# Norm statistics on 32 partitions per block of 128 tokens, with an early table load and one rounding moved

## What is computed

```python
def layer_norm(x, g, b):
    mu = jnp.mean(xf, axis=-1, keepdims=True)
    var = jnp.mean(jnp.square(xf - mu), axis=-1, keepdims=True)
    return (xf - mu) * lax.rsqrt(var + LN_EPS) * g + b

def rms_norm_2(x, g):
    return xf * lax.rsqrt(jnp.mean(xf * xf, axis=-1, keepdims=True) + RMS_EPS) * g

# first stack, for each of 2 layers
x = layer_norm(ALPHA * x + token_mixing(x), ln1_g[l], ln1_b[l])
x = layer_norm(ALPHA * x + conv_ffn(x), ln2_g[l], ln2_b[l])

# second stack, for each of 2 layers
x = x + rms_norm_2(mixer(rms_norm_2(x, g[0])), g[1])
x = x + rms_norm_2(mem_cross_attention(rms_norm_2(x, g[2]), mem_n), g[3])
x = x + rms_norm_2(sqrelu_mlp(rms_norm_2(x, g[4])), g[5])
```

## Time and profile before

| what | us |
|---|---|
| median of 3 runs (3763.27 to 3771.85) | 3764.62 |
| profiled execution, its own time | 3758.41 |
| span of the profiled execution | 3756.6 |
| busy: PE / DVE / ACT / POOL in that span | 3638.1 / 1692.9 / 1495.7 / 1276.3 |

### The profile page before, as it was taken

One profiled execution on the slowest core, in us unless ns is written; L12 is line 12 of the kernel. 1 busy time (PEld: TensorE's weight loads), 2 busy tenths in 40 slices (PEclk: granted clock), 3 DMA queues, 4 the chain that ended last, 5 costly groups with the idle time before them and its releaser, 6 DMA issues.

```text
span 3756.6 us, 47739 instructions
## 1 busy us (share of the span) xinstructions
PE 3638.1 (97%) x17594; PEld 2844.2 (76%) x17594; DVE 1692.9 (45%) x2392; ACT 1495.7 (40%) x2452; POOL 1276.3 (34%) x583
## 2 busy tenths in 40 slices
PE   8999999999999999999999999999999999999997
PEld 7877787888788777778877676888744587777886
DVE  2633457443344443754325643503247564436042
ACT  3256633332323664243325544423225144344232
POOL 4422233444343222444443142444200012433442
PEclk9999999999999999999999999999999999999999
DMA  3421122223233111222222221222322200212222
GB/s 139 124 68 51 46 76 77 99 96 101 91 104 113 48 49 51 96 81 98 99 99 94 101 96 62 93 98 95 102 90 72 75 2 30 95 68 84 100 96 78
DMA packets 100867, 313.06 MB, mean 83 GB/s; under 512 B 26208, under 2 KB 26336, under 8 KB 99808
## 3 DMA queue, kind: packets, MB, share of 16 engines
q1 hardware_dynamic: 81792, 298.90, 23.6%
q10 hardware_dynamic: 18912, 11.88, 1.3%
HBM read 302.35 MB, written 5.24 MB: 82 GB/s over the span
## 4 chain that ended last, share of the span: by engine, by line
issue 45%; PE 35%; POOL 16%; DVE 2%; DMA 1%; ACT 1%; DVEq 0%; POOLq 0%; SPq 0%; ACTq 0%
POOL ring_r L2748 16%; PE ps L456 9%; PE ps L458 9%; PE ps L457 9%; PE ps L978 2%; PE ps L1078 1%; PE ps L812 1%; PE ps L997 1%; DMA ring<-in_weights 1%; PE ps L1114 0%; PE ps L1217 0%; PE ps L1166 0%; PE ps L1216 0%; DVE rounded L2646 0%; DVE Z L2646 0%
## 5 line engine op out<-in xcount | busy, mean ns | idle before, releaser
L2748 POOL TENSOR_TENSOR ring_r<-ring,rounded_r 128x1024 fp32r<-128x1024 f32 x504 | 1238.1, 2459 | 2026.1 <-ACT rounded_r L1268 2025.9
L456 PE MATMUL ps<-source_hi,rounded_r 128*128 128x512 f32 x2560 | 1015.7, 397 | 45.8 <-DVE N_lo L2326 11.1
L1268 ACT ACTIVATE rounded_r<-ring 128x1024 fp32r<-128x1024 f32 x504 | 533.5, 1059 | 1309.7 <-PE ps L458 1177.3
L457 PE MATMUL ps<-source_hi,ring_r 128*128 128x512 f32 x2560 | 1001.2, 391 | 0.0
L456 PEld LDWEIGHTS ps<-source_hi,rounded_r 128*128 128x128 f32 x2560 | 483.4, 189 | 170.0 <-DVE N_lo L2326 19.3
L458 PE MATMUL ps<-X_lo,rounded_r 128*128 128x512 f32 x1536 | 600.3, 391 | 0.0
L457 PEld LDWEIGHTS ps<-source_hi,ring_r 128*128 128x128 f32 x2560 | 483.9, 189 | 100.2 <-issue 2.4
L458 PEld LDWEIGHTS ps<-X_lo,rounded_r 128*128 128x128 f32 x1536 | 289.5, 188 | 61.0
L458 PE MATMUL ps<-N_lo,rounded_r 128*128 128x512 f32 x768 | 300.8, 392 | 0.0
L2291 DVE SCALAR_TENSOR_TENSOR T<-ps,PAR,T 128x511 f32<-128x511 f32 (+1 forms) x176 | 131.5, 749 | 227.5 <-ACT T L1483 212.6
L456 PE MATMUL ps<-H_hi,rounded_r 128*128 128x512 f32 x512 | 199.2, 389 | 0.0
(11 more groups left out here) (506 smaller groups left out, 5540.2 us busy)
## 6 DMA issues: line engine op xcount, KB each, us to landing
ring<-in_weights SPq DMA_DIRECT2D x560, 512.0 KB, 3.3
X<-in_x SPq DMA_DIRECT2D x2, 1024.0 KB, 7.0
PAIR<-Z ACTq DMA_DIRECT2D x32, 64.0 KB
out_x<-X SPq DMA_DIRECT2D x4, 512.0 KB, 2.6
SWAP<-Z ACTq DMA_DIRECT2D x4, 256.0 KB, 6.1
MEM<-in_mem ACTq DMA_DIRECT2D x1, 1024.0 KB, 4.7
mem_keys<-Z ACTq DMA_DIRECT2D x1, 1024.0 KB, 3.9
diag_in<-Y ACTq DMA_DIRECT2D x8, 128.0 KB, 2.6
```

The source lines that it names most:

```text
L456: mm(o, lh, rh, start=start, stop=False)
L457: mm(o, ll, rh, start=False, stop=False)
L1268: av(RH[:, j, :], ring[:, j, :], ACT.Copy).then_inc(w_hi, 1)
L2748: nc.gpsimd.tensor_tensor(RL[:, j, :], ring[:, j, :], RH[:, j, :].bitcast(F32), ALU.subtract).then_inc(w_lo, 1)
```

## The change

A new helper `by_block` takes the place of one matmul with 512 columns by four with 128 columns: block b of 128 tokens goes through a 128x32 part of the matrix of means to output partitions 32b to 32b+31, columns 0 to 127. The statistics then lie as 128x128 from the start. `from_block` is the loop that `spread` had, with a bank as argument.

- Layer norm: the mean is summed twice, whole in bank 4 (for `less`) and by blocks in bank 7; the mean of squares is summed by blocks in bank 5. ScalarE squares 128x128, VectorE subtracts in one instruction. `warm(7, 3)` becomes `warm(6, 2)`. One `less` moves ahead of the reciprocal.
- Output norm: sums by blocks, root and reciprocal on 128x128, and a new step `rms_spread` on TensorE whose 128x512 result stays in PSUM (bank 5 or 0), where `residual` reads it instead of `RS` in SBUF. It stands behind `values(0)` for 2 and 8, behind one `warm` for 4 and 10 (four matmuls of `warm` instead of six), behind the first chunk of keys for 6, and at the end for 12.
- Layer norm on ScalarE: the root of one element that brings the table comes ahead of square 5 instead of square 7, and the rounding of the chunk for slot 2 comes behind the square of the mean instead of ahead of it.

```diff
+            def by_block(bank, src, start, stop):
+                for b in range(ST):
+                    ins = mm(ps[b * 32:b * 32 + 32, bank, 0:P], cst("mean")[:, 0:32], src[:, b * P:b * P + P], start=start, stop=stop)
+                return ins
+            def from_block(bank):
+                for b in range(ST):
+                    row = cst("ident")[:, b * 32:b * 32 + 1].to_broadcast([P, P])
+                    ins = mm(ps[:, bank, b * P:b * P + P], row, RS[:, 0:P], start=True, stop=True)
+                return ins
             def sums(l, i):
                 mm(ps[:, 4, :], cst("mean"), RS[:], start=True, stop=False)
+                by_block(7, RS[:], True, False)
...
-                mm(ps[:, 5, :], cst("mean"), QSUM, start=True, stop=False)
+                by_block(5, QSUM, True, False)
             def sums_of(l, i, n):
-                ins = mm(ps[:, 4, :], cst("mean"), X[:, n, :], start=False, stop=last)
+                ins = by_block(7, X[:, n, :], False, last)
                 if last:
                     ins.then_inc(ln["sums"], 1)
+                mm(ps[:, 4, :], cst("mean"), X[:, n, :], start=False, stop=last)
...
-                ins = mm(ps[:, 5, :], cst("mean"), SQ[n % 2], start=False, stop=last)
+                ins = by_block(5, SQ[n % 2], False, last)
...
             def rms_out(i):
-                mm(ps[:, 5, :], cst("mean"), QS, start=True, stop=False)
+                by_block(5, QS, True, False)
                 pe.wait_ge(rms_sq, i * KT + KT)
-                mm(ps[:, 5, :], cst("mean"), SQ2[(KT - 1) % 2], start=False, stop=True).then_inc(rms_var, 1)
+                by_block(5, SQ2[(KT - 1) % 2], False, True).then_inc(rms_var, 1)
+            def rms_spread(i):
+                pe.wait_ge(rms_inv, OUT_AT[i] + 1)
+                from_block(OUT_BANK[i]).then_inc(rms_fac, 1)
...
             def squared(l, i, n):
-                if n == KT - 1:
+                if n == KT - 3:
                     av(JUNK[:], cst("eps"), ACT.Sqrt)
...
             def layer_norm(l, i, bias, following):
-                av(SQ[KT % 2], ps[:, 4, :], ACT.Square).then_inc(s["act"], 1)
+                av(SQ[KT % 2][:, 0:P], ps[:, 7, 0:P], ACT.Square).then_inc(s["act"], 1)
+                ahead(slot // RING, slot % RING)
...
-                for b in range(ST):
-                    rows, t = slice(b * 32, b * 32 + 32), slice(b * P, b * P + P)
-                    ins = tt(QSUM[rows, 0:P], ps[rows, 5, t], SQ[KT % 2][rows, t], ALU.subtract)
-                ins.then_inc(s["dve"], 1)
+                tt(QSUM[:, 0:P], ps[:, 5, 0:P], SQ[KT % 2][:, 0:P], ALU.subtract).then_inc(s["dve"], 1)
+                less(0)
                 dve.wait_ge(s["act"], at * LN_ACT + LN_STD)
                 v.reciprocal(RS[:, 0:P], RS[:, 0:P]).then_inc(s["dve"], 1)
-                less(0, 1)
+                less(1)
...
             def residual(i, lo=None):
-                inverse_root(i)
+                dve.wait_ge(rms_std, i + 1)
+                v.reciprocal(RS[:, 0:P], RS[:, 0:P]).then_inc(rms_inv, 1)
+                dve.wait_ge(rms_fac, OUT_AT[i] + 1)
...
-                        tt(N[:, t, :], N[:, t, :], RS[:], ALU.mult)
+                        tt(N[:, t, :], N[:, t, :], ps[:, OUT_BANK[i], :], ALU.mult)
```

More of the change, by code:

```diff
@@ L552, in spread @@
                 pe.wait_ge(ln["dve"], (l * 2 + i) * LN_DVE + LN_ROOT)
-                for b in range(ST):
-                    row = cst("ident")[:, b * 32:b * 32 + 1].to_broadcast([P, P])
-                    ins = mm(ps[:, 6, b * P:b * P + P], row, RS[:, 0:P], start=True, stop=True)
-                ins.then_inc(ln["sums"], 1)
+                from_block(6).then_inc(ln["sums"], 1)
             def scores(l, u):
@@ L861, in values @@
                     ins.then_inc(used, 1)
-                for c in range(RING):
+                values(0)
+                rms_spread(2 + 6 * l)
+                for c in range(1, RING):
                     values(c)
@@ L1494, in _ @@
                         squared(l, 1, c // 3)
-                    ahead(Q + (B_DOWN + c) // RING, c % RING)
+                    if c < C_DOWN - 1:
+                        ahead(Q + (B_DOWN + c) // RING, c % RING)
                     if c == 3 * RING - 1:
@@ L1628, in tail @@
                 out_tiles(B + B_MO, 4 + 6 * l, gain(l, 3), 4)
-                root(4 + 6 * l)
+                root(4 + 6 * l, 5, P)
                 split_in(2 + 3 * l, gain(l, 4))
@@ L1669, in tail @@
                                 av(N[:, n, :], N[:, n, :], ACT.Copy, scale=gain(l, 5)[:, n:n + 1])
-                root(6 + 6 * l)
+                root(6 + 6 * l, 5, P)
             act.dma_start(MN, a["mem"]).then_inc(mem_in, 16)
@@ L1745, in _ @@
             out_tiles(B_LRU_OUT, 2, gain(0, 1), bias="b_out")
-            root(2)
+            root(2, 5, P)
             tail(0)
@@ L1965, in _ @@
             out_tiles(B_RWO, 8, gain(1, 1))
-            root(8)
+            root(8, 5, P)
             tail(1)
```

19 lines of the change are left out of this document (13 added, 6 removed).

## The result

The changed kernel takes 3741.68 us (median of 4 runs, 3740.17 to 3743.55), the kernel before 3763.94 us in the runs beside it (4 runs, 3762.69 to 3771.85): ratio 0.9937, 95% interval 0.9919 to 0.9954. The profiled executions differ by less: span 3741.7 against 3756.6, that is 14.9.

The account below looks back on a forecast made before the run. TensorE, busy 97% of the span, bounds the kernel, so only its waits and unneeded work at norms count. Savings 5.0 + 2.6 + 2.6 + 1.8 = 12.0 us give 3746.4 profiled, median 3752.6; range 3746.5 to 3762.

Parts of the forecast that it names:

- The price of a group: TensorE: a `by_block` group of eight 128-column passes costs 0.25 us, four parts at a time; rivals 0.50 (0.20), 1.00 (0.10).
- a change of shape: TensorE: switching between whole matmuls and groups costs 0.10 us each time.
- Layer norms: Four layer norms: reciprocal about 3.0 behind the last tile, saving 1.7 each behind mixing, 0.8 each behind feed-forward; 5.0 us.
- The 0.88 that I put down to the table load: Layer norms behind the mixing: the last square sits out the table load, so the reciprocal starts 0.88 us later than behind feed-forward.
- The moved rounding: Layer norms, ScalarE: the 1.04 us rounding, put behind the square of the mean, is just covered ahead of the root.
- Norm 12, norms 4 and 10: Output norms: first tile sooner by 2.6 us at norm 12 and by 1.32 each at 4 and 10, together 2.6.
- 1.41: Output norms 12, 4 and 10: us taken from the reciprocal through the spread to the first tile.
- Norms 2 and 8: Output norms 2 and 8: between 0 and 1.8 us each, middle 0.9 taken, together 1.8.
- The collisions: Norms 2 and 8: VectorE waits for GpSimd where two inputs are in SBUF, so part of the gain is given back.
- Norm 6: Output norm 6: keys keep TensorE busy, the spread adds 1.0 us and the groups save 1.0, so 0.
- a saving is the same in the profiled execution and in the median: Whole kernel: the median stays 6.2 us above the profiled execution, so the 12.0 saved counts equally in both.
- a chance of 0.07 for the better side: Clock rival: stretches at the lower clock level vanish as waits ahead of the product get shorter; 3748 us, chance 0.07.

Follow-up runs that it names:

- e5: Changed kernel with extra unread matmuls ahead of norm 12's sums: four groups on four array places, four on one, four whole matmuls; 0.90, 3.58 and 3.63 us.
- e11: Kernel before with only the table load and the rounding moved as in the change, sums whole as before; 3758.81 us, ratio 0.9997.
- e6: Changed kernel with the table load put back ahead of the last square; 3743.18 us, ratio 0.9958.
- e7: Changed kernel with the rounding of the last chunk back ahead of the square of the mean; 3741.97 us, ratio 0.9954.
- e9: Changed kernel with output norms 2 and 8 put back as before; 3745.67 us, ratio 0.9960.
- e12: Changed kernel with two warming matmuls instead of one ahead of the spread at norms 4 and 10; 3744.42 us, ratio 0.9958.
- e16: As e14, but in the layer norms the last chunk's rounding stands ahead of the root, as in the change; 3743.86 us, ratio 0.9951.
- e17: Changed kernel with the last chunk's rounding behind the root at norms 4 and 10 alone; 3743.12 us, ratio 0.9953.
- e13: Changed kernel, layer norms reordered: whole mean summed last, roundings behind the root, reciprocal ahead of both `less`, one warming matmul fewer; 3746.26 us, ratio 0.9966.
- e14: As e13, and at norms 4 and 10 the last chunk's rounding stands behind the root; 3745.24 us, ratio 0.9964.
- e1: Kernel before, unedited, run again against itself; 3761.62 us, ratio 0.9998.
- e2: Changed kernel, unedited, run again against the kernel before; 3739.87 us, ratio 0.9944.
- e15: Changed kernel, unedited, run a third time against the kernel before; 3742.96 us, ratio 0.9955.
- e8: Kernel before with eight warming matmuls instead of six behind output norms 4 and 10; 3762.30 us, ratio 1.0007.

## Why the prediction was too small

- **The price of a group** was right: 0.25 forecast, 0.23 in e5. A group and a whole matmul in turn take 0.35 + 1.06, against 0.23 + 0.91 each among its like (e5), so a change of shape costs 0.13, where the earlier trace rows gave 0.10. The Trainium skill, TensorEngine Tiling (Array Packing), Key Properties, says that a change of tiling mode drains TensorE; the rows agree that a change costs time.
- **Layer norms**, forecast 5.0, measured 5.9. The reciprocal starts 2.83 behind the last tile, not 3.0, since the instructions of VectorE ahead of it overlap by 0.1 each; the rest is that the product follows 4.62 behind the reciprocal, before 4.70. The 0.88 that I put down to the table load is there with whole sums (e11); once TensorE's whole mean stands between the last two groups it is 0.17 at the reciprocal, and 0.57 at the product by way of GpSimd (e6), a path that the prediction did not have. The moved rounding is worth nothing (e7).
- **Norm 12, norms 4 and 10**, forecast 2.6 and 2.6, measured 2.9 and 3.3. The steps were right. From the reciprocal's end through the spread to the first tile I took 1.41, where a step of `less` stood in between; here it is 1.26. The root takes 0.37.
- **Norms 2 and 8**, forecast 0.9 each, measured 1.45. The bounds (0 to 1.8) held; the middle was too careful. The collisions fall on other instructions, with about the same sum, and do not eat the gain.
- **Norm 6**, forecast 0, measured 0.25.
- **The step that failed most** is the sentence that a saving is the same in the profiled execution and in the median. It put the median 6.2 above the profiled execution's own time; with the change it lies 1.9 below (3741.68 and 3743.55). That is 8.1 of the 10.9 between forecast and result; the other 2.8 is the profiled execution itself, 3743.55 where 3746.4 was forecast. The runs show most of what is behind the 8.1. The 3764.62 shown was 4.2 above the mean of 79 runs (3760.4), and the changed kernel's runs had a mean clock 0.0015 higher than theirs, 2.8. With 3.2 from the terms and 0.7 left over that is the 10.9 again. I had looked for the clock only behind the norms, in stretches of 1.7 each, with a chance of 0.07 for the better side; runs of one and the same kernel spread by 13 us, much of it with the clock, and the range left 6 us below the forecast. That the terms were 3.2 too small would not have put the time out of the range.

What stays open is whether the changed kernel's higher clock belongs to it. It had 0.9928 in 14 runs, but its near relatives e6, e7, e9, e12, e16 and e17 0.9916 to 0.9924, e13 and e14 0.9908 and 0.9898, and the kernel before 0.9905 to 0.9921 by series. The profiled executions show no such difference ahead of norm 12: 47.8 and 41.0 us at the lower level before (the first profile and e1), 41.0, 47.8 and 41.0 in the changed kernel (the first, e2, e15). Behind norm 12's sums the last stretch is 1.0 to 1.8 us shorter, as the tail is, which makes 0.0002 of the 0.0015 at most. Filling the waits behind norms 4 and 10 did not raise the mean clock (e8).

## What to carry to other kernels

Measure a change by its places: from a fixed event to a fixed event the lengths mostly repeat within 0.1 us, while runs differ by several. Before a median of few runs is taken as the start of a forecast, look at the clock of each run. And where two engines run side by side into one subtraction, price a part by what it has over the other engine after the whole change, not before it, and up to the next product: a step that is 0.17 late may make GpSimd late, and the product 0.57.

## What the runs showed of the hardware that I had not expected

- Four 128x32 parts of the array take fp32 passes side by side without loss: 0.225 us for 8 passes of 128 columns, against 0.90 on one part (e5).
- A run's time follows its mean granted clock with 1.9 us for 0.001. If all of the lost clock were work of TensorE on the path it would be 3.8 (0.001 of 3757); half of it arrives.
- A reciprocal 0.74 us sooner made the next product 0.9 later (e13), since a rounding on ScalarE, moved past one root, started GpSimd at the moment at which VectorE needed two inputs from SBUF.
